# Token halves at the turn from one residual stage to the next stage's first products, in a two-layer decoder trunk on one Trainium2 core

## The chip, the cores and the metric

The kernel runs on one core of a Trainium2 chip. Its time is the device time of that core, in microseconds (us). Five engines take part, each with its own instruction order and joined by semaphores: PE (TensorE, the matmuls), ACT (ScalarE), VectorE (DVE), POOL (GpSimd) and SP (SyncE, which issues the DMAs).

## What is computed

512 tokens of 1024 features pass through two layers. Each layer has a token mixer (an HGRN2 gated recurrence, then FoX, attention with a forget gate) and an MLP with squared ReLU, each between a conditioned norm and a gated residual update:

```python
def rmsnorm(x, w):
    return x * lax.rsqrt(jnp.mean(x * x, axis=-1, keepdims=True) + EPS) * w
def modulate(x, w, shift, scale):
    return rmsnorm(x, w) * (1 + scale) + shift
# layer i
h = modulate(x, norm1_w[i], sh1, sc1)
y = hgrn2_mixer(h, ...) if i % 2 == 0 else fox_mixer(h, ...)      # ends in "@ w_out"
x = x + g1 * y
h = modulate(x, norm2_w[i], sh2, sc2)
a = relu(h @ w1[i]); x = x + g2 * ((a * a) @ w2[i])               # 4096 wide inside
# at the end
rmsnorm(x, final_w)
```

## The kernel before

**Layout.** Everything between stages is feature-major: x holds 8 tiles (k = 0 to 7) of 128 features by 512 tokens. Each product is made in three matmuls of fp32r, from an upper and a lower part of either side (upper by upper, upper by lower, lower by upper; `product`, L620, the matmuls at L624 to L626).

**Weights.** All large weights lie in one stream of 208 blocks of 128 x 1024 values, four blocks to a quad. A quad's block j has slot j of three buffers: `raw` (filled by SP, L233), `whi` (the upper part, made by ACT in `hi_ahead`, L283 to L287) and `wlo` (raw less whi, made by POOL in `lo`, L544 to L547). `hi_ahead(quad, j)` waits until PE is through with block j of that quad (`pe_blk`) and until raw holds block j of the next one; `lo` waits for it, SP reloads raw behind `lo`, and PE's `split` (L617) waits for both parts. Layer 0 has quads 0 to 25 and layer 1 quads 26 to 51: 8 for the mixer's input, 2 for w_out, 16 for the MLP. The MLP goes in two halves of four quads w1 and four quads w2, so that in the second half the last four quads (12 to 15 of the MLP) are w2. A w_out tile takes one block, a w2 tile takes two.

**Residual stage.** With each tile that PE finishes, VectorE updates x from the PSUM bank (L1178), ACT squares the tile into `sqb` (L380) and VectorE adds it to `acc` (L1188); PE's next use of the bank waits for the update (`x_upd`). ACT's `residual` (L370) does, for each quad:

```python
for j in range(4):
    if not last and j < 3:
        hi_ahead(q0 + q, j)
    if j % per == per - 1:      # per: blocks a tile, 1 at w_out, 2 in the MLP
        ...                     # square of the tile
    if not last and j == 3:
        hi_ahead(q0 + q, j)
```

**Norm.** After the last tile `norm` of PE (L636) sums acc and the last square over the features with a column of 1/1024 (L641, L646). VectorE adds epsilon (L997), POOL takes the power -1/2 (L551), PE spreads it over the partitions (L651). Then, tile by tile, VectorE scales x into one of two buffers (L1008), ACT adds the shift and rounds to the upper part (L293) and VectorE makes the lower part (L1013). PE's next products start with each k as it lands: `together` (L704) takes two blocks at once, FoX alternates the forget gate's product (L936 to L938) with token blocks of 256 columns (L679 to L681). There are five norms; norm 0 is at the start, 1 and 3 follow w_out, 2 and 4 the MLPs. Norm 4 is the last: VectorE scales x in place (L1339) and SP stores each tile (L277).

**Behind norm 2.** The forget gate's product is followed by ACT's absolute value, exponential and logarithm (L414 to L418), VectorE's scan (L1236), and the trip of the result through DRAM. In ACT's order the weights' upper parts for FoX's next blocks stand behind this. q and k are squared, summed over a head (L1242), rooted on POOL (L551) and scaled (L1253) before PE turns them (L879) and begins the scores (L894).

## Time and profile before

| | us |
|---|---|
| median of 3 runs | 1496.41 |
| lowest and highest | 1494.38, 1497.65 |
| span of the profiled execution | 1490.3 |
| PE busy in it | 1416.5 (95%) |
| VectorE busy | 753.5 (51%) |
| POOL busy | 687.3 (46%) |
| ACT busy | 506.8 (34%) |

The profile gives the span from the first to the last instruction of one execution; that execution's own time is not listed beside it, so the median is read as 6.1 us above the span. Busy PE is not PE at its peak, since matmuls overlap: what counts is the distance from one start to the next. A matmul row shows its start, its duration with the drain, the line, and the tiles it writes and reads; "x8" merges eight alike. The bracket at a row's end is how long the engine had been idle and what released it.

### The profile page before, as it was taken

What the parts mean: (1) busy time and instruction counts of PE and PEld (TensorE: products, weight loads), DVE (VectorE), ACT (ScalarE), POOL (GpSimd) and SP (SyncE); (2) the same over time, 40 slices, a digit from 0 to 9 for tenths busy, and PEclk for the clock granted to TensorE, in tenths of its full rate; (3) what the DMA queues carried; (4) which work ended last, traced back from release to release, by engine and by line L of the source; (5) the groups of instructions that cost most, each with busy time, mean ns of one, the idle gap of its engine ahead of it and who ended that gap; (6) DMA issues with size and microseconds to landing.
All of it is one profiled execution on the core that took longest, in us unless ns stands there. A gap on an engine that the chain in (4) does not pass through costs nothing.

```text
span 1490.3 us, 20799 instructions
## 1 busy us (share of the span) xinstructions
PE 1416.5 (95%) x7488; PEld 1186.5 (80%) x7488; DVE 753.5 (51%) x1087; ACT 506.8 (34%) x750; POOL 687.3 (46%) x399
## 2 busy tenths in 40 slices
PE   2789999999899999999998999999989999999997
PEld 2678988988788888888787888888778888888885
DVE  7764656464698457871253333333356541255312
ACT  3513232313343223332245353534234332233220
POOL 8456758474355455554434333333053444444440
PEclk9889999999899999999999999999999999999998
DMA  9233433322265456542323121211032223222221
GB/s 380 101 141 114 141 114 118 137 72 70 87 225 197 169 181 214 197 165 89 99 68 103 57 86 57 86 58 57 15 104 80 89 95 99 85 99 99 85 70 57
DMA packets 46192, 169.83 MB, mean 114 GB/s; under 512 B 5024, under 2 KB 5152, under 8 KB 45360
## 3 DMA queue, kind: packets, MB, share of 16 engines
q1 hardware_dynamic: 45520, 164.73, 32.0%
q10 hardware_dynamic: 608, 4.23, 0.8%
q8 instruction: 43, 0.70, 0.2%
q14 instruction: 21, 0.17, 0.0%
HBM read 166.81 MB, written 2.13 MB: 113 GB/s over the span
## 4 chain that ended last, share of the span: by engine, by line
PE 66%; issue 19%; POOL 8%; DVE 5%; ACT 1%; DMA 1%; POOLq 0%; DVEq 0%; ACTq 0%; SPq 0%
PE bank L624 13%; PE bank L625 13%; PE bank L626 13%; POOL wlo L547 8%; PE bank L679 4%; PE bank L681 4%; PE bank L680 4%; PE bank L752 3%; PE bank L894 3%; PE bank L918 2%; PE bank L771 1%; PE bank L905 1%; DVE modf L1073 1%; PE bank L896 1%; DVE mring L1033 1%
## 5 line engine op out<-in xcount | busy, mean ns | idle before, releaser
L547 POOL TENSOR_TENSOR wlo<-raw,whi 128x1024 fp32r<-128x1024 f32 x208 | 539.2, 2596 | 661.5 <-ACT whi L287 661.5
L287 ACT ACTIVATE whi<-raw 128x1024 fp32r<-128x1024 f32 x204 | 215.1, 1055 | 211.3 <-PE bank L626 187.5
L1178 DVE SCALAR_TENSOR_TENSOR x<-bank,mod,x 128x512 f32<-128x512 f32 (+1 forms) x48 | 35.9, 749 | 234.6 <-PE bank L626 234.6
L1033 DVE CUSTOM_DVE_ANT_0 mring<-mring,cb 128x1024 f32<-128x1024 f32 x80 | 124.9, 1570 | 4.0 <-DMA mring<-mod_rows 4.0
L679 PE MATMUL bank<-whi,h2hi 128*128 128x256 f32 x384 | 111.3, 290 | 0.0
L1266 DVE CUSTOM_DVE_ANT_0 scr<-bank,fb 128x128 f32<-128x128 f32 (+1 forms) x64 | 31.1, 486 | 153.7 <-issue 153.7
L681 PE MATMUL bank<-wlo,h2hi 128*128 128x256 f32 x384 | 108.5, 283 | 0.0
L680 PE MATMUL bank<-whi,h2lo 128*128 128x256 f32 x384 | 108.4, 282 | 0.0
L398 ACT ACTIVATE scr<-bank 128x512 f32<-128x512 f32 x64 | 38.2, 597 | 196.4 <-PE bank L626 196.4
L624 PE MATMUL bank<-h3hi,whi 128*128 128x512 f32 x256 | 102.1, 399 | 2.4 <-issue 2.4
L624 PE MATMUL bank<-h1hi,whi 128*128 128x512 f32 x256 | 100.9, 394 | 2.4 <-DVE h1lo L1013 2.4
L625 PE MATMUL bank<-h3lo,whi 128*128 128x512 f32 x256 | 101.7, 397 | 0.0
L626 PE MATMUL bank<-h3hi,wlo 128*128 128x512 f32 x256 | 101.7, 397 | 0.0
L625 PE MATMUL bank<-h1lo,whi 128*128 128x512 f32 x256 | 101.3, 396 | 0.0
L625 PE MATMUL bank<-a1lo,whi 128*128 128x512 f32 x256 | 101.0, 395 | 0.0
L624 PE MATMUL bank<-a1hi,whi 128*128 128x512 f32 x256 | 101.0, 395 | 0.0
L626 PE MATMUL bank<-a1hi,wlo 128*128 128x512 f32 x256 | 101.0, 395 | 0.0
L624 PE MATMUL bank<-a0hi,whi 128*128 128x512 f32 x256 | 100.7, 393 | 0.3
L626 PE MATMUL bank<-h1hi,wlo 128*128 128x512 f32 x256 | 100.8, 394 | 0.0
L625 PE MATMUL bank<-a0lo,whi 128*128 128x512 f32 x256 | 100.1, 391 | 0.0
L626 PE MATMUL bank<-a0hi,wlo 128*128 128x512 f32 x256 | 99.9, 390 | 0.0
L624 PE MATMUL bank<-h0hi,whi 128*128 128x512 f32 x192 | 81.7, 426 | 15.6 <-DVE h0lo L1013 15.3
(231 smaller groups left out, 3158.3 us busy)
## 6 DMA issues: line engine op xcount, KB each, us to landing
raw<-stream SPq DMA_DIRECT2D x208, 512.0 KB, 3.5
mring<-mod_rows SPq DMA_DIRECT2D x80, 512.0 KB, 3.5
modf<-mod_rows SPq DMA_DIRECT2D x8, 1024.0 KB, 18.1
fb<-negf ACTq DMA_DIRECT2D x4, 1024.0 KB, 5.5
x<-x_t SPq DMA_DIRECT2D x2, 1024.0 KB, 7.0
out_t<-x SPq DMA_DIRECT2D x8, 256.0 KB, 2.1
cb<-c_row SPq DMA_DIRECT2D x1, 512.0 KB, 4.1
wf<-w_forget SPq DMA_DIRECT2D x1, 512.0 KB, 4.3
```

Of the source, the lines that this page charges most:

```text
L287: S.activation(whi[:, j, :], raw[:, j, :], ACT.Copy).then_inc(w_hi, 1)
L398: S.activation(scr[j % 2][:, :], ps[j][:, :], ACT.Relu).then_inc(ff_r, 1)
L547: G.tensor_tensor(wlo[:, j, :], raw[:, j, :], whi[:, j, :].bitcast(F32), ALU.subtract).then_inc(w_lo, 1)
L624: PE.matmul(out, wh, hh[0], start=first, stop=False)
L625: PE.matmul(out, wh, hh[1], start=False, stop=False)
L626: return PE.matmul(out, wl, hh[0], start=False, stop=last)
L679: PE.matmul(o, hh, whi[:, j, w0], start=k == 0 and t % 2 == 0, stop=False, skip_group_check=True)
L680: PE.matmul(o, hl, whi[:, j, w0], start=False, stop=False, skip_group_check=True)
L681: mm = PE.matmul(o, hh, wlo[:, j, w0], start=False, stop=k == KT - 1, skip_group_check=True)
L752: mm = PE.matmul(second_halves(cols(ps[j], t), m), cols(kk, t), second_halves(cols(qq, t), m), start=True, stop=True)
L894: PE.matmul(o[:, 0:n], qkT[0][r:r + DH, f, P * i:P * i + P], qkT[1][r:r + DH, f, 0:n], start=True, stop=False, skip_group_check=True)
L1033: V.tensor_tensor_reduce(out=mring[:, s, :], in0=mring[:, s, :], in1=cb[:, :], scale=1.0, scalar=0.0, op0=ALU.mult, op1=ALU.add, accum_out ...
```

## The change

In each of the four turns (n = 1 to 4, after w_out and MLP of each layer) the last quad of the residual stage runs twice over its four blocks, first for tokens 0 to 255, then for tokens 256 to 511. Norm n is done by such halves (`sums`, `spread`, `variance`, `half_root`, `normed_tokens`); the sums and the spread of half 0 stand inside the last quad's second round, those of half 1 inside the first quad of the next stage, which also goes by token halves. Scaled tiles have four buffers of 256 tokens. The last norm's output is stored in pairs of half tiles. The squares of the MLPs' first halves, which were summed and never used, are gone, and so are the memsets of `acc`: the first square of a stage is written into it. ACT's and VectorE's `residual` and `norm` become a `turnover` each, written out, where ACT's order of weight conversions and squares is new. In SBUF h1 now lies ahead of a0, and h2 ahead of FoX's other tiles.

```diff
+        h1 = [sb(n, [P, KT, T], F32R, mlp0) for n in ("h1hi", "h1lo")]
         a0 = [sb(n, [P, HALF, T], F32R, mlp0) for n in ("a0hi", "a0lo")]
-        h1 = [sb(n, [P, KT, T], F32R, mlp0) for n in ("h1hi", "h1lo")]
         wf = sb("wf", [P, D], F32, mlp0)
...
         fox = ExitStack()
+        h2 = [sb(n, [P, KT, T], F32R, fox) for n in ("h2hi", "h2lo")]
...
+        OUT_UPD, MLP_UPD, LAST_UPD = 12, 8, 10
+        UPD_AT = [0, 12, 20, 30, 42, 50]
...
-                sp.wait_ge(out_t_ready, k + 1)
-                sp.dma_start(out_t[:, k, :], x[:, k, :]).then_inc(out_done, 16)
+            for th in range(2):
+                for k in range(0, KT, 2):
+                    sp.wait_ge(out_t_ready, KT * th + k + 2)
+                    sp.dma_start(out_t[:, k:k + 2, part(th)], x[:, k:k + 2, part(th)]).then_inc(out_done, 16)
             sp.wait_ge(out_done, 16 * KT)
 
...
+            def upper(n, th, first, end, h, shift):
+
+                for k in range(first, end):
+                    act.wait_ge(h_t, h_at(n, th, k))
+                    S.activation(h[0][:, k, part(th)], t_buf(th, k), ACT.Identity,
                                  bias=mod[:, shift + k:shift + k + 1]).then_inc(h_hi, 1)
...
+            def square(n, upd, i, add, t, cols_, dst):
+
+                act.wait_ge(x_upd, upd)
+                act.wait_ge(x_acc, add)
+                S.activation(dst[:, cols_], x[:, t, cols_], ACT.Square).then_inc(x_sq, 1)
+
+            def square_half(n, th, t):
+
+                r, full_ = (0, 4) if from_w_out(n) else (2, 6)
+                upd = UPD_AT[r + 3 * (n > 2)] + full_ + (KT - full_) * th + t - full_ + 1
+                add = ADD_AT[n] + full_ - 1 + (KT - full_ - 1) * th + t - full_
+                square(n, upd, 0, add, t, part(th), sqb)
 
             act.wait_ge(c_in, 16)
...
+            def turnover(n, q0, h, shift):
+
+                all_ = slice(0, T)
+                if from_w_out(n):
                     for j in range(4):
...
+                        hi_ahead(q0, j)
+                        square(n, UPD_AT[3 * (n > 2)] + j + 1, 0, ADD_AT[n] + max(j - 1, 0), j, all_, sqb if j else acc)
+                    q0 += 1
+                else:
+                    for t in range(6):
+                        square(n, UPD_AT[2 + 3 * (n > 2)] + t + 1, 0, ADD_AT[n] + max(t - 1, 0), t, all_, sqb if t else acc)
+                        if t % 2:
+                            for j in ((0, 1, 2, 3)):
+                                hi_ahead(q0 + t // 2, j)
+                    q0 += 3
+                last_ = range(4, KT) if from_w_out(n) else range(6, KT)
+                for t in last_:
+                    square_half(n, 0, t)
+                if from_w_out(n):
+                    for j in range(2):
+                        square_half(n, 1, 4 + j)
+                        hi_ahead(q0, j)
+                    upper(n, 0, 0, 3, h, shift)
+                    square_half(n, 1, 6)
+                    hi_ahead(q0, 2)
+                    upper(n, 0, 3, 6, h, shift)
+                    square_half(n, 1, 7)
+                    hi_ahead(q0, 3)
+                else:
+                    if n == 4:
+                        square_half(n, 1, 6)
+                        square_half(n, 1, 7)
+                        return
+                    hi_ahead(q0, 0)
+                    square_half(n, 1, 6)
+                    hi_ahead(q0, 1)
+                    upper(n, 0, 0, 3, h, shift)
+                    hi_ahead(q0, 2)
+                    upper(n, 0, 3, 6, h, shift)
+                    square_half(n, 1, 7)
+                    hi_ahead(q0, 3)
+                upper(n, 0, 6, KT, h, shift)
+                upper(n, 1, 0, KT, h, shift)
...
+                    if half == 0:
+                        with act.Fori(0, 4) as q:
+                            for j in range(4):
+                                hi_ahead(q + base + 4, j)
+                turnover(2 * layer + 2, base + 12, h, shift)
+
...
+            def half_root(n, th):
+
+                root(n_var, norm_at(n, th), 2, n_rst, 2 * th)
+
             def lo_quads(first, end, n):
 
                 with pool.Fori(first, end - 1) as q:
                     for j in range(4):
                         lo(q, j)
+                half_root(n, 0)
                 for j in range(4):
-                    if j == 3:
-                        root(n_var, n, TT, n_rst)
                     lo(end - 1, j)
-
-            lo_quads(Q_OUT + 1, Q_OUT + 3, 2)
-            lo_quads(Q_MLP + 1, LAYER_QUADS + 1, 3)
+                half_root(n, 1)
...
+            def half_block(quad, j, out, h, th, k0=0, first=True, last=True, between=None):
+
+                if th == 0:
+                    split(quad, j)
+                for k in range(KT):
+                    mm = product(out[:, part(th)], j, k, [h[0][:, k0 + k, part(th)], h[1][:, k0 + k, part(th)]],
+                                 first and k == 0, last and k == KT - 1)
+                    if between is not None and k in between:
+                        between[k]()
+                return mm
+
...
+            def sums(n, th):
+
+                bank = ps[SUMS_BANK[n][th]]
+                pe.wait_ge(x_acc, adds_at(n, th))
+                pe.wait_ge(x_sq, squares_at(n, th))
+                for i in range(2):
+                    PE.matmul(bank[:, i:i + 1], cols(acc, 2 * th + i), meand[:, 0:1], start=i == 0, stop=False,
+                              skip_group_check=True)
+                for i in range(2):
+                    mm = PE.matmul(bank[:, i:i + 1], cols(sqb, 2 * th + i), meand[:, 0:1], start=False, stop=True,
+                                   skip_group_check=True)
+                mm.then_inc(n_sum, 1)
+
+            def spread(n, th):
+
+                bank = ps[SPREAD_BANK[n][th]]
+                pe.wait_ge(n_rst, norm_at(n, th))
+                for i in range(2):
+                    mm = PE.matmul(cols(bank, i), rst[:, 2 * th + i:2 * th + i + 1].broadcast_to([P, P]), ident[:, :],
+                                   start=True, stop=True)
...
+            def w_out(quad, y, y_done, upd0, n):
                 pe.wait_ge(*y_done)
                 for j in range(4):
                     for k in range(EARLY, KT):
                         mm = product(ps[4 + j][:, :], j, k, [y[0][:, k, :], y[1][:, k, :]], False, k == KT - 1)
                     mm.then_inc(pe_blk, 1)
                 for j in range(4):
+                    half_block(quad + 1, j, ps[j], y, 0).then_inc(pe_half, 1)
+                for j in range(4):
                     pe.wait_ge(x_upd, upd0 + j + 1)
-                    feature_block(quad + 1, j, 4 + j, y)
+                    between = {5: lambda: sums(n, 0)} if j == 0 else None
+                    half_block(quad + 1, j, ps[4 + j], y, 1, between=between).then_inc(pe_blk, 1)
+                    if j == 1:
+                        pe.wait_ge(x_upd, upd0 + 9)
+                        spread(n, 0)
 
...
+                            for pair in range(2):
+                                for k in range(KT):
+                                    if pair == 0:
+                                        pe.wait_ge(h_lo, h_at(n, th, k))
+                                    for j in (2 * pair, 2 * pair + 1):
+                                        if th == 0 and k == 0:
+                                            split(base, j)
+                                        mm = product(ps[j][:, part(th)], j, k, [h[0][:, k, part(th)], h[1][:, k, part(th)]],
+                                                     k == 0, k == KT - 1)
+                                        if th == 1 and k == KT - 1:
+                                            mm.then_inc(pe_blk, 1)
+                                    if th == 0 and k == 3:
+                                        (sums, spread)[pair](n, 1)
                         first = 1
                     with pe.Fori(first, 4) as q:
...
-            w_out(Q_OUT, y0, (y_lo, KT), 0)
-            norm(1)
+                quad, n = base + 15, 2 * layer + 2
+                for th in range(2):
+                    for j in range(4):
+                        out = ps[(0, 6)[th] + j // 2]
+                        between = {5: lambda: sums(n, 0)} if th and j == 0 else None
+                        mm = half_block(quad, j, out, a, th, k0=KT * (j % 2), first=j % 2 == 0, last=j % 2 == 1,
+                                        between=between)
+                        if th:
+                            mm.then_inc(pe_blk, 1)
+                        elif j % 2:
+                            mm.then_inc(pe_half, 1)
+                        if th and j == 1:
+                            spread(n, 0)
...
+            def token_half(n, bank, th, k):
+
+                j = (n + k // 4) % 4
+                if th == 0 and k % 4 == 0:
+                    split((n + k // 4) // 4, j)
+                w0 = slice(GW * (k % 4), GW * (k % 4) + GW)
+                for t in (2 * th, 2 * th + 1):
+                    o = ps[bank + th][:, GW * (t % 2):GW * (t % 2) + GW]
+                    hh, hl = cols(h2[0][:, k, :], t), cols(h2[1][:, k, :], t)
+                    PE.matmul(o, hh, whi[:, j, w0], start=k == 0 and t % 2 == 0, stop=False, skip_group_check=True)
+                    PE.matmul(o, hl, whi[:, j, w0], start=False, stop=False, skip_group_check=True)
+                    mm = PE.matmul(o, hh, wlo[:, j, w0], start=False, stop=k == KT - 1, skip_group_check=True)
+                if th and k % 4 == 3:
+                    mm.then_inc(pe_blk, 1)
...
-                for k in (2 * kk, 2 * kk + 1):
-                    pe.wait_ge(h_lo, 2 * KT + k + 1)
+            for th in range(2):
+                for k in range(KT):
+                    pe.wait_ge(h_lo, h_at(2, th, k))
+                    token_half(4 * L, 4, th, k)
                     wh, wl = cols(wfs[0], k), cols(wfs[1], k)
-                    PE.matmul(ps[0][:, :], wh, h2[0][:, k, :], start=k == 0, stop=False)
-                    PE.matmul(ps[0][:, :], wh, h2[1][:, k, :], start=False, stop=False)
-                    mm = PE.matmul(ps[0][:, :], wl, h2[0][:, k, :], start=False, stop=k == KT - 1)
-                if kk == KT // 2 - 1:
+                    PE.matmul(ps[0][:, part(th)], wh, h2[0][:, k, part(th)], start=k == 0, stop=False)
+                    PE.matmul(ps[0][:, part(th)], wh, h2[1][:, k, part(th)], start=False, stop=False)
+                    mm = PE.matmul(ps[0][:, part(th)], wl, h2[0][:, k, part(th)], start=False, stop=k == KT - 1)
+                    if th == 0 and k == 3:
+                        sums(2, 1)
+                if th:
                     mm.then_inc(f_pe, 1)
-                fox_half(-1, 4 + kk)
-            for i in range(8, 16):
+                for k in range(KT):
+                    token_half(4 * L + 2, 6, th, k)
+                    if th == 0 and k == 1:
+                        spread(2, 1)
+            for i in range(12, 16):
...
+            def variance(n, th):
+
+                dve.wait_ge(n_sum, norm_at(n, th))
+                eps_var(ps[SUMS_BANK[n][th]][:, 0:2], 2, 2 * th).then_inc(n_var, 1)
+
+            def normed_tokens(n, th, first, end, h, shift):
+
+                if first == 0:
+                    dve.wait_ge(n_bc, norm_at(n, th))
+                for k in range(first, end):
+                    if KT * th + k >= 4:
+                        dve.wait_ge(h_lo, h_at(n, th, k) - 4)
+                    V.scalar_tensor_tensor(out=t_buf(th, k), in0=x[:, k, part(th)],
+                                           scalar=gain[:, KT * n + k:KT * n + k + 1],
+                                           in1=ps[SPREAD_BANK[n][th]][:, 0:TH], op0=ALU.mult, op1=ALU.mult).then_inc(h_t, 1)
+                for k in range(first, end):
+                    dve.wait_ge(h_hi, h_at(n, th, k))
+                    V.scalar_tensor_tensor(out=h[1][:, k, part(th)], in0=t_buf(th, k),
+                                           scalar=mod[:, shift + k:shift + k + 1],
+                                           in1=h[0][:, k, part(th)].bitcast(F32), op0=ALU.add,
+                                           op1=ALU.subtract).then_inc(h_lo, 1)
...
+            def update(t, bank, cols_, gate):
+
+                V.scalar_tensor_tensor(out=x[:, t, cols_], in0=ps[bank][:, cols_], scalar=mod[:, gate + t:gate + t + 1],
+                                       in1=x[:, t, cols_], op0=ALU.mult, op1=ALU.add).then_inc(x_upd, 1)
+
+            def added(square_at, cols_):
+
+                dve.wait_ge(x_sq, square_at)
+                V.tensor_tensor(acc[:, cols_], acc[:, cols_], sqb[:, cols_], ALU.add).then_inc(x_acc, 1)
+
+            def turnover(n, q0, gate, half0, h, shift):
+
+                all_ = slice(0, T)
+                full_ = 4 if from_w_out(n) else 6
+                per = 1 if from_w_out(n) else 2
+                for t in range(full_):
+                    dve.wait_ge(pe_blk, 4 * q0 + per * (t + 1))
+                    update(t, 4 + t % (4 // per), all_, gate)
+                    if t:
+                        added(SQ_AT[n] + t + 1, all_)
+                for t in range(full_, KT):
+                    dve.wait_ge(pe_half, half0 + t - full_ + 1)
+                    update(t, t - full_, part(0), gate)
+                    if t < KT - 1:
+                        added(SQ_AT[n] + t + 1, part(0))
+
+                def second(t):
+                    dve.wait_ge(pe_blk, 4 * q0 + per * (t + 1))
+                    update(t, (4 if from_w_out(n) else 6) + t - full_, part(1), gate)
+                    if t < KT - 1:
+                        added(SQ_AT[n] + KT + t - full_ + 1, part(1))
+
+                variance(n, 0)
+                if n == 4:
+                    second(6)
+                    finished(0)
+                    second(7)
+                    variance(n, 1)
+                    finished(1)
+                    return
+                if from_w_out(n):
+                    second(4)
+                    second(5)
+                else:
+                    second(6)
+                normed_tokens(n, 0, 0, 3, h, shift)
+                if from_w_out(n):
+                    second(6)
+                normed_tokens(n, 0, 3, 6, h, shift)
+                second(7)
+                normed_tokens(n, 0, 6, KT, h, shift)
+                variance(n, 1)
+                for k in range(0, KT, 2):
+                    normed_tokens(n, 1, k, k + 2, h, shift)
```

## Rows read from the trace of the kernel before

**Rows 1.** Windows of layer 1's MLP; busy us and instructions of each engine, then clock, DMA
```profile
1140.00:1450.00 310.00, 310.00 (x1336) 251.34 (x1335) 119.49 (x87) 97.11 (x128) 134.52 (x57) 1.00 0.28 92
```

**Rows 2.** PE's timeline after w_out of layer 0: start us, us, line, operands
```profile
378.07 0.95 PE L641 MATMUL bank<-meand,acc 128*128 128x1 f32 x8
...
382.29 2.07 PE L651 MATMUL bank<-ident,rst 128*128 128x128 f32 x8 [1.34 <-POOL rst L551]
386.75 0.80 PE L624 MATMUL bank<-h1hi,whi 128*128 128x512 f32 x1 [2.38 <-DVE h1lo L1013]
...
391.13 0.39 PE L625 MATMUL bank<-h1lo,whi 128*128 128x512 f32 x1
...
399.84 0.39 PE L624 MATMUL bank<-h1hi,whi 128*128 128x512 f32 x1
```

**Rows 3.** PE's timeline after w_out of layer 1
```profile
1109.24 0.94 PE L641 MATMUL bank<-meand,acc 128*128 128x1 f32 x8
...
1113.47 1.16 PE L651 MATMUL bank<-ident,rst 128*128 128x128 f32 x8 [1.34 <-POOL rst L551]
1117.06 0.76 PE L624 MATMUL bank<-h3hi,whi 128*128 128x512 f32 x1 [2.43 <-issue]
```

**Rows 4.** Timeline at the end of layer 0's MLP
```profile
741.21 0.95 PE L641 MATMUL bank<-meand,acc 128*128 128x1 f32 x8
741.41 0.75 DVE L1178 SCALAR_TENSOR_TENSOR x<-bank,mod,x 128x512 f32<-128x512 f32 x1 [6.90 <-PE bank L626]
```

**Rows 5.** PE's timeline from there to FoX's first scores
```profile
749.49 0.77 PE L936 MATMUL bank<-h2hi,wfhi 128*128 128x512 f32 x1 [2.47 <-DVE h2lo L1013]
...
768.18 0.28 PE L679 MATMUL bank<-whi,h2hi 128*128 128x256 f32 x1
...
774.06 0.28 PE L680 MATMUL bank<-whi,h2lo 128*128 128x256 f32 x1
...
796.05 0.46 PE L894 MATMUL bank<-kT,qT 64*128 64x128 f32 x2 [0.87 <-ACT kT L455]
```

**Rows 6.** Timeline at the span's end, PE and VectorE
```profile
1476.11 0.95 PE L641 MATMUL bank<-meand,acc 128*128 128x1 f32 x8
...
1480.17 2.08 PE L651 MATMUL bank<-ident,rst 128*128 128x128 f32 x8 [1.34 <-POOL rst L551]
...
1482.29 5.36 DVE L1339 SCALAR_TENSOR_TENSOR x<-x,par,bank 128x512 f32<-128x512 f32 x8 [2.71 <-PE bank L651]
```

**Rows 7.** Timeline between two quads of layer 0's second w2 half
```profile
719.23 0.39 PE L624 MATMUL bank<-a0hi,whi 128*128 128x512 f32 x1
...
719.65 0.75 DVE L1178 SCALAR_TENSOR_TENSOR x<-bank,mod,x 128x512 f32 x1 [7.11 <-PE bank L626]
...
720.61 0.63 ACT L380 ACTIVATE sqb<-x 128x512 f32 x1 [5.61 <-DVE x L1178]
...
721.15 1.04 ACT L287 ACTIVATE whi<-raw 128x1024 fp32r<-128x1024 f32 x1
...
722.27 2.42 POOL L547 TENSOR_TENSOR wlo<-raw,whi 128x1024 fp32r<-128x1024 f32 x1 [4.80 <-ACT whi L287]
```

**Rows 8.** VectorE's groups by form: xcount, busy us, mean ns, idle before
```profile
L1188 DVE TENSOR_TENSOR acc<-acc,sqb 128x512 f32<-128x512 f32 x44 | 59.3, 1349 | 32.6 <-ACT sqb L380 32.6
...
L1178 DVE SCALAR_TENSOR_TENSOR x<-bank,mod,x 128x512 f32<-128x512 f32 x24 | 17.9, 747 | 69.1 <-PE bank L626 69.1
...
L1275 DVE COPY pT<-bank 128x512 f32<-128x512 f32 x16 | 11.1, 692 | 4.9 <-PE bank L905 3.2
...
L1275 DVE COPY pT<-bank 128x256 f32<-128x256 f32 x16 | 6.7, 420 | 0.0
```

**Rows 9.** VectorE's timeline, FoX's first quads, then the kernel's start
```profile
777.39 5.69 DVE L1253 TENSOR_TENSOR qt<-qt,rst 128x512 f32<-128x512 f32 x2 [3.02 <-POOL rst L551]
...
40.60 2.14 DVE L1013 SCALAR_TENSOR_TENSOR h0lo<-scr,mod,h0hi 128x512 fp32r<-128x512 f32 x1
```

**Rows 10.** POOL's timeline behind the forget gate
```profile
771.11 3.23 POOL L547 TENSOR_TENSOR wlo<-raw,whi 128x1024 fp32r<-128x1024 f32 x1 [23.41 <-ACT whi L287]
```

197 lines of the change are left out of this document (82 added, 115 removed).

## Prediction

> **What bounds the kernel now.** The page and the windows by stage come first: in a long stretch of the MLPs PE is busy in all 310 us of 310, so there only PE's own work counts. [rows 1] PE stands still elsewhere: at the four places where a residual stage ends and a norm stands between it and the next product, so I read PE's timeline around each. After w_out of layer 0 the last long matmul gives way to the sums at 378.07, the spread runs at 382.29, the first product of the norm's output starts at 386.75, and the first two blocks end at 399.84. [rows 2] Two blocks of 24 matmuls at 0.229 us are 11.0 us, so 21.8 - 11.0 = 10.8 us are lost: 8.7 us of gap, and about 2 us since ten matmuls from 386.75 on take 4.4 us for 2.3 (a granted clock of 1.2 instead of 2.4 GHz). After w_out of layer 1 the gap is 7.8 us and the loss, with the same slow restart, about 10.0. [rows 3] After the MLP of layer 0 the gap is 8.3 us. [rows 4, 5] The last norm has nothing behind it: from 1476.11 to the span's end are 14.2 us. [rows 6] These four losses are all that the split of the last quad can win.
>
> **What the change does to PE's work.** A block of 24 matmuls of 512 columns becomes 48 of 256: 8 blocks at each w_out turn, 5 at the first MLP's (the forget gate's product counts as one), 4 at the end, 25 in all, 600 pairs. Matmuls of 256 columns (FoX's token blocks) start every (774.06 - 768.18) / 49 = 0.120 us [rows 5], so a pair costs 0.240 for 0.229: 600 x 0.011 = 6.6 us more. The Trainium skill (TensorE: Matmul & The Clock Gate, section Back-to-back issue gap) gives columns / 2.4 GHz plus 2.5 ns between matmuls; by that the split would cost 600 x 2.5 ns = 1.5 us, and I go by the rows. Sums (8 short matmuls) and spread (4) now stand in PE's stream, 0.84 + 0.49 us a half by their pitch of 0.105 and 0.12; they are in the schedules below. That a0 and h1 trade places, and h2 moves, I cost at nothing: they keep the token half that is being written off tiles still read, and the pitch is 0.229 whichever tile streams.
>
> **The step that decides: weights behind the odd squares.** ScalarE rounds each raw block into its upper part (hi_ahead), POOL then makes the lower one, and a slot can be refilled once PE has read it. Before, hi_ahead of slots 0 to 2 runs right after each block, with three blocks of cover. In the new ACT turnover of the MLPs, the loop over t = 0 to 5 takes the square of t first and converts all four slots only if t is odd, (0, 1, 2, 3). Square 1 waits for update 1, which waits for the fourth block of the quad. So no slot of the next quad is started before this quad is wholly done, and its block 0 has no cover. The trace has this very chain, for the slot that came last: PE goes on to the next quad at 719.23, update 719.65, square 720.61, upper part 721.15, lower part 722.27 to 724.69: 5.5 us. [rows 7] There it delayed nothing, since slot 3 is needed 16 us later; now slot 0 is behind it and PE waits. In code without the loop's register work the update starts 0.20 us after PE, not 0.42 [rows 4], so I take 5.3. The other slots follow every 2.4 us and PE needs one every 5.5, or 2.9 in halves, so it is one wait a quad: before quads 13, 14 and 15 of each MLP, 6 x 5.3 = **31.8 us**. The bounds are 5.0 and 5.6 (30 and 34 in all): no row lets the chain be shorter. The clock: at two of three turns it was down 4.1 to 4.2 us after the last long matmul (8 spreads took 2.07 and 2.08 us, at the third 1.16) [rows 2, 3, 6], and a restart then cost 2.1 us; while here PE has not even the short matmuls in between. I take 1.5 us a wait, nearer to that row than to nothing, **9.0** in all, between 0 and 13.
>
> **The four turns, worked as a schedule.** Halved durations are the 512-wide ones less 0.27 on VectorE, as its copies of 512 and 256 columns show (0.692 and 0.420 us) [rows 8]: update, scaling and lower part 0.48 us, addition 0.43. Square 0.42 is an estimate, a third off the 0.63 of rows 7, less than VectorE's copies lose; upper part 0.51 and root 0.69 likewise, and an error of 0.1 in each moves a turn by 0.3. Added to it is a collision. VectorE instructions that read two SBUF tensors wait while POOL makes a lower part: additions mean 1.35 us for 0.69 alone, two adjacent multiplies took 5.69 together for 1.4, room for two lower parts by POOL of 2.4 each ahead of them, and a lower part of h0 took 2.14 for 0.75. Updates, which read PSUM and SBUF, never do (mean 0.75). [rows 8, 9] The new order puts POOL's four lower weights (2.4 us each) among VectorE's lower halves of h. With T the start of the second halves of a w_out turn: sums of half 0 at T + 2.2, root 3.4, spread after block 1 at 6.6. The lower part of k = 0 waits behind POOL until 11.4, just in time for PE at 12.9. Then k = 3 is behind POOL's third block (14.9 to 17.3) and lands at 17.7, when PE has been idle since 15.0; the sums of half 1 wait for the last square until 19.8; k = 6 is behind POOL's fourth (to 23.1) and lands at 23.6. The second token half is in time. In all 6.4 us idle and 48.7 of work, 55.1 us from the start of the last quad to the end of the next stage's first quad. Before: 22.0 + 10.8 + 22.0 = 54.8. So **+0.3** at the first turn, and against 54.0 **+1.1** at layer 1's: the norm's gap is given back.
>
> After layer 0's MLP the products end at 57.1 after the quad's start, for 60.5 before. But the forget gate's product now ends with the second token half, at 51.4 instead of 46.1. Behind it are ScalarE's two table loads, the upper part for the next block, VectorE's scan and POOL's lower part, which ended at 774.34, 55.1 after the quad's start. [rows 10] Shifted by 5.3 it is ready at 60.4: PE waits from 57.1. The normalised q, ready at 783.1 (63.8) [rows 9], comes at 69 and PE wants it at 66; k's follows. The first scores, at 796.05 or 76.8 before [rows 5], start at 81.5: **+4.7**.
>
> At the end, half 0's scaling is hidden, half 1 goes through update, square, sums, root, spread and eight scalings of 0.40: the last ends 31.7 after the quad's start. Before it was 22.0 + 11.5; from there to the span's end 2.65 us stay (the stores' bytes are the same). [rows 6] 34.4 for 36.2: **-1.8**.
>
> **Edits costed at nothing.** The MLPs' first halves lose eight squares and additions a layer, and the memsets of acc go: work of ACT and VectorE beside a PE that doesn't wait there [rows 1], so no gain either. SP issues as many stores as before, eight of two tiles' halves in place of eight whole tiles, and its raw loads keep their place behind the lower parts; a raw slot has the rest of a quad, over 16 us, to fill, and if that were gone PE would wait for the load as well. POOL runs each root ahead of the lower weights that follow it; the roots are short, and VectorE's variance ahead of them doesn't wait for those weights.
>
> **Sum.** 31.8 + 9.0 + 0.3 + 1.1 + 4.7 - 1.8 = 45.1 us. The profiled execution's span of 1490.3 becomes 1535.4; the median of the three runs, 6.1 above that span, becomes 1541.5.
>
> **Rivals.**
> 1. The clock does not fall in the six waits: 1541.5 - 9.0 = 1532.5. For it: after layer 1's w_out the spread, 4.2 us in, still ran at the full clock (8 matmuls in 1.16 us) [rows 3]. Against: 2.07 and 2.08 us for the same 8 at two other turns. [rows 2, 6] Chance 0.22.
> 2. The collision with POOL does not bite (it finds gaps between VectorE's shorter instructions). The same schedules without it give 48.9 for the w_out turns, 73.0 for the scores: -5.9 - 5.1 - 3.8 - 1.8 = -16.6 instead of +4.3, so 1520.6. Against it are rows that show the very pair of operations. [rows 8, 9] Chance 0.14.
> 3. Not slower: the conversion before each quad is hidden after all. With rival 2's turns at -16.6, it decides from the point where the six waits and their clock cost under 2.8 us each; at nothing the time is 1479.8. That needs ACT to convert slot 0 before square 1, which the order of its instructions forbids. Chance 0.04.
> 4. The clock stays down through the halved blocks too, a fall costing 3 us instead of 1.5 and one more of 2 at each of three turns: +9 and +6, 1556.5. Chance 0.08.
>
> **Numbers.** Forecast 0.52, the rivals as above. The range takes in rivals 1 and 2 and the forecast's own bounds (the waits at 5.6, the clock at 13): 1520 to 1553. About 0.2% is what a measurement of this kernel can tell from no change: faster 0.03, same 0.01, slower 0.96.
>
> **What would show it.** Right: six gaps of PE of 5.0 to 5.6 us in the second halves of the MLPs, ended by POOL's wlo, each some 22 us after the last, and a granted clock below 1 in the slices around; at the w_out turns gaps of 1 to 3 us ended by the lower parts of h while POOL is busy; the first block after the forget gate held by wlo. Wrong: no wait of PE for wlo at those quads, or a norm turn shorter than before by 5 us.

## The result, and the profile after

The median of four runs after is 1536.20 us (1534.91 to 1538.62), of four runs before 1497.02: ratio 1.0264, 95% interval 1.0245 to 1.0284, so 39 us slower. The forecast was 1541.5 in a range of 1520 to 1553. The profiled execution took 1534.91 us, its span 1532.9: 42.6 us more than the span before. The span is what is split up here; that it grew by 3 us more than the median comes from the trace before, as e8_places will show.

Windows of the changed kernel over its two second w2 halves, from the first quad to the end of the halved quad's first round. Columns as in [rows 1].

```profile
653.00:753.00 100.00, 84.94 (x397) 71.08 (x396) 15.01 (x23) 17.79 (x23) 31.21 (x13) 0.91 0.23 72
1410.00:1511.00 101.00, 86.08 (x399) 71.65 (x398) 12.38 (x16) 17.47 (x22) 30.49 (x13) 0.92 0.16 51
```

Where PE was busy all the time at a clock of 1.00 [rows 1], it now stands still for 15 us in each stretch, at a mean granted clock of 0.91 and 0.92. The page's groups of instructions name what ended that idle time, the same for both layers:

```profile
L704 PE MATMUL bank<-a0hi,whi 128*128 128x512 f32 (+1 forms) x288 | 109.4, 380 | 15.2 <-POOL wlo L622 14.9
L704 PE MATMUL bank<-a1hi,whi 128*128 128x512 f32 (+1 forms) x288 | 109.5, 380 | 14.9 <-POOL wlo L622 14.9
```

The timeline at the first of the six places, quad 12 to quad 13 of layer 0:

```profile
673.71 0.39 PE L706 MATMUL bank<-a0hi,wlo 128*128 128x512 f32 x1
674.14 0.75 DVE L1335 SCALAR_TENSOR_TENSOR x<-bank,mod,x 128x512 f32<-128x512 f32 x1 [10.23 <-PE bank L706]
674.92 0.63 ACT L336 ACTIVATE sqb<-x 128x512 f32<-128x512 f32 x1 [10.35 <-DVE x L1335]
675.46 3.88 ACT L323 ACTIVATE whi<-raw 128x1024 fp32r<-128x1024 f32 x4
...
676.58 7.00 POOL L622 TENSOR_TENSOR wlo<-raw,whi 128x1024 fp32r<-128x1024 f32 x3 [20.07 <-ACT whi L323]
679.07 0.76 PE L704 MATMUL bank<-a0hi,whi 128*128 128x512 f32 x1 [4.97 <-POOL wlo L622]
...
679.63 0.63 PE L705 MATMUL bank<-a0lo,whi 128*128 128x512 f32 x1
...
683.90 0.62 PE L706 MATMUL bank<-a0hi,wlo 128*128 128x512 f32 x1
684.33 0.43 PE L704 MATMUL bank<-a0hi,whi 128*128 128x512 f32 x1
684.59 0.39 PE L705 MATMUL bank<-a0lo,whi 128*128 128x512 f32 x1
```

It is the chain of [rows 7], now for all four slots: the quad's last matmul, update, square, then four upper parts in a row, and PE goes on once the first lower part is made. From start to start 5.36 us lie between the two matmuls, 0.23 of it the matmul itself: 5.13 us lost. Behind the wait eleven matmuls start 0.43 us apart instead of 0.23, the lower of the clock's two levels, and cost 2.5 us more. The six waits are 5.13 or 5.14 us each; their slow matmuls cost 2.5, 1.4 and 2.3 us in layer 0, 2.6, 1.4 and 2.1 in layer 1, 12.4 us in all. After the middle wait of each layer some 5 matmuls were slow, after the others 10 or more.

PE's timeline can be cut into stretches, each around one turn; their lengths in us:

| stretch | before | after | difference |
|---|---|---|---|
| n=1: w_out of layer 0 to the first product over a | 129.0 | 127.4 | -1.6 |
| n=2: layer 0's second w2 half to the first scores | 143.1 | 166.9 | +23.8: waits 15.4, their clock 6.3, the turn +2.1 |
| FoX: first scores to w_out | 282.4 | 283.3 | +0.8 |
| n=3: w_out of layer 1 to the first product over a | 129.9 | 129.0 | -0.9 |
| n=4: layer 1's second w2 half to the span's end | 103.4 | 123.7 | +20.3: waits 15.4, their clock 6.1, the turn -1.3 |

With 0.3 us ahead of the first of them, that makes the 42.6. The rest of the MLPs is unchanged.

VectorE, POOL and PE after w_out of layer 0. The kernel before has no counterpart, since its norm stood alone there:

```profile
376.23 2.41 POOL L622 TENSOR_TENSOR wlo<-raw,whi 128x1024 fp32r<-128x1024 f32 x1 [0.43 <-ACT whi L323]
377.18 2.54 DVE L1188 SCALAR_TENSOR_TENSOR h1lo<-scr,mod,h1hi 128x256 fp32r<-128x256 f32 x3
...
381.59 2.36 POOL L622 TENSOR_TENSOR wlo<-raw,whi 128x1024 fp32r<-128x1024 f32 x1 [2.95 <-ACT whi L323]
382.11 2.91 DVE L1188 SCALAR_TENSOR_TENSOR h1lo<-scr,mod,h1hi 128x256 fp32r<-128x256 f32 x3
384.28 0.38 PE L704 MATMUL bank<-h1hi,whi 128*128 128x256 f32 x1 [1.83 <-DVE h1lo L1188]
```

Each time VectorE's group of three ends 1.1 us after POOL's block (378.64 to 379.72, 383.95 to 385.02), two lower parts' time or a little more: so the first one ends about when the block does, and PE waits for it. PE's line at the turn after layer 0's MLP:

```profile
798.31 0.55 PE L791 MATMUL bank<-whi,h2hi 128*128 128x256 f32 x1 [3.27 <-POOL wlo L622]
...
816.96 0.66 PE L1017 MATMUL bank<-ident,kt 128*128 128x128 f32 x4 [3.24 <-DVE kt L1467]
818.48 0.76 PE L1032 MATMUL bank<-kT,qT 64*128 64x128 f32 x2 [0.87 <-ACT kT L531]
```

### The profile page after: what moved, and what is told of

Its sections match the earlier page's. It is cut to its first block, busy times and chain, and to the rows that moved or that the text cites. A ratio compares the mean times of both kernels' runs of the same rounds, so it can differ in the third digit from the quotient of the medians.

```text
span 1532.9 us, 21793 instructions
## 1 busy us (share of the span) xinstructions
PE 1432.9 (93%) x8088; PEld 1224.4 (80%) x8088; DVE 739.6 (48%) x1136; ACT 501.5 (33%) x770; POOL 690.6 (45%) x403
## 4 chain that ended last, share of the span: by engine, by line
PE 41%; issue 33%; POOL 16%; DVE 7%; ACT 2%; DMA 1%; POOLq 0%; DVEq 0%; SPq 0%; ACTq 0%
POOL wlo L622 15%; PE bank L704 6%; PE bank L706 6%; PE bank L705 6%; PE bank L791 3%; PE bank L793 3%; PE bank L792 3%; PE bank L864 3%; PE bank L1032 3%; PE bank L1056 2%; PE bank L883 1%; PE bank L1043 1%; DVE modf L1239 1%; PE bank L1034 1%; DVE h2lo L1188 1%
## 5 line engine op out<-in xcount | busy, mean ns | idle before, releaser
L704 PE MATMUL bank<-a0hi,whi 128*128 128x512 f32 (+1 forms) x288 | 109.4, 380 | 15.2 <-POOL wlo L622 14.9
L704 PE MATMUL bank<-a1hi,whi 128*128 128x512 f32 (+1 forms) x288 | 109.5, 380 | 14.9 <-POOL wlo L622 14.9
L704 PE MATMUL bank<-h3hi,whi 128*128 128x512 f32 (+1 forms) x288 | 107.5, 373 | 2.2 <-DVE h3lo L1188 2.1
L704 PE MATMUL bank<-h1hi,whi 128*128 128x512 f32 (+1 forms) x288 | 107.1, 372 | 2.2 <-DVE h1lo L1188 2.1
L705 PE MATMUL bank<-a1lo,whi 128*128 128x512 f32 (+1 forms) x288 | 108.7, 377 | 0.0
L706 PE MATMUL bank<-a1hi,wlo 128*128 128x512 f32 (+1 forms) x288 | 108.7, 377 | 0.0
L706 PE MATMUL bank<-a0hi,wlo 128*128 128x512 f32 (+1 forms) x288 | 107.9, 375 | 0.0
L705 PE MATMUL bank<-a0lo,whi 128*128 128x512 f32 (+1 forms) x288 | 107.7, 374 | 0.0
L706 PE MATMUL bank<-h3hi,wlo 128*128 128x512 f32 (+1 forms) x288 | 107.0, 371 | 0.0
L705 PE MATMUL bank<-h3lo,whi 128*128 128x512 f32 (+1 forms) x288 | 106.9, 371 | 0.0
```

Source lines behind the costliest of these rows:

```text
L704: PE.matmul(out, wh, hh[0], start=first, stop=False)
L705: PE.matmul(out, wh, hh[1], start=False, stop=False)
L706: return PE.matmul(out, wl, hh[0], start=False, stop=last)
```

## Experiments on the six waits

**e1_order.** Only the order of ScalarE in the MLPs' turnover is put back:

```diff
 for t in range(6):
+    for j in ((0, 1), (2,))[t % 2]:
+        hi_ahead(q0 + t // 2, j)
     square(...)
-    if t % 2:
-        for j in ((0, 1, 2, 3)):
-            hi_ahead(q0 + t // 2, j)
+    for j in ((), (3,))[t % 2]:
+        hi_ahead(q0 + t // 2, j)
```

> The changed kernel with one thing put back: in the six early squares of each MLP's turnover, ScalarE makes the upper parts of slots 0 and 1 ahead of the even square, that of slot 2 ahead of the odd one and that of slot 3 behind it. Theory A (this order alone makes the six waits of PE, and the clock's fall behind them is part of their price): the trace of the changed kernel has 6 x 5.13 = 30.8 us of gap before quads 13, 14 and 15 of each MLP and 12.5 us of slow matmuls behind them, so 1536.2 - 43.3 = 1493, that is 3 to 4 us under the kernel before; no gap of PE for wlo there. Theory B (the raw blocks or POOL's queue are late as well, and the order only showed it first): waits of 1 us or more stay at these quads, and the time is over 1500.

Measured: 1494.15 us, ratio to before 0.9985 (0.9972 to 0.9998): 42 of the 43 us are back, and the kernel is 1.7 us under the one before that ran beside it, where 3 to 4 were expected. The windows of the same two stretches:

```profile
653.00:731.00 78.00, 77.86 (x393) 65.86 (x392) 19.03 (x23) 18.92 (x23) 32.38 (x13) 1.00 0.30 93
1390.00:1469.00 79.00, 79.00 (x396) 66.51 (x395) 15.73 (x16) 17.92 (x22) 31.20 (x13) 1.00 0.20 63
```

PE is busy throughout at a clock of 1.00. All the rest of the change (halves, norms within products, places) is worth 0.15%, with an interval from 0.02 to 0.28.

**e2_slot0.** As above, but with `((0,), ())` ahead of the square and `((), (1, 2, 3))` behind it.

> The changed kernel with only slot 0's upper part made early (ahead of the even square); slots 1 to 3 are still made behind the odd square, when the quad is done. Theory A (one wait a quad, slot 0's; the later slots have blocks of PE's in front of them): slot 1's lower part lands 5.1 us after the quad, as slot 0's did; PE wants it after 5.5 us in whole blocks (no wait) and after 2.8 us in the halved last quad (a wait of 2.3 us, twice), so some 5 us more than with the whole order put back, plus a clock fall of up to 2 us each: 1493 + 5 to 9 = 1498 to 1502. Theory B (the wait moves to slot 1 in every quad, since POOL and the clock are as late as before): three quarters or more of the loss stays, 1525 or more.

Measured: 1498.11 us, 1.0014 (1.0004 to 1.0024), 4.0 us over e1_order. PE's timeline has no wait before quads 13 and 14, and in the halved quad one at slot 1:

```profile
725.20 0.36 PE L705 MATMUL bank<-a0hi,whi 128*128 128x256 f32 x1 [2.26 <-POOL wlo L623]
```

By the starts that is 2.41 us, and 2.29 at the same place of layer 1, against 2.3 expected: a wait is 5.1 us less the cover that the slot has, 0 for slot 0, 2.8 or 5.5 us for slot 1.

**e3_old_late.** The kernel before, with both squares of the three inner quads ahead of all four `hi_ahead`.

> The kernel before, with whole quads and whole norms, in which the three inner quads of each MLP's second w2 half make the upper parts of all four slots behind both squares. Theory A (the order alone, whatever the halves do): six waits of 5.1 to 5.3 us, 31 us, and the slow matmuls behind them, 12 us: 1497 + 43 = 1540, slower than the changed kernel itself by the 3 to 4 us that the halves win. Theory B (the halved last quads or the moved tiles have a part in the waits or in the clock's fall): 1497 + 20 to 30, under 1530.

Measured: 1542.26 us, 1.0296 (1.0273 to 1.0319). One of its six waits:

```profile
681.74 0.77 PE L637 MATMUL bank<-a0hi,whi 128*128 128x512 f32 x1 [5.38 <-POOL wlo L560]
```

With the loop's register work ahead of the update each wait is 5.5 us, as [rows 7] had it; the slow matmuls cost 1.8, 2.5 and 2.8 us in layer 0, 1.4, 2.1 and 2.5 in layer 1. The kernel is 46 us over the one before that ran beside it, where 43 were expected. The loss needs nothing of the halves.

**e4_filled.** The changed kernel; at the end of each quad of the second w2 half:

```diff
+if half:
+    pe.wait_ge(x_upd, q * 2 + (UPD_AT[3 * layer + 2] + 1))
+    for _ in range(20):
+        PE.matmul(ps[4][:, :], a[0][:, 0, 0:P], a[0][:, 0, :], start=True, stop=True)
```

> The changed kernel, in which PE runs 20 matmuls of 512 columns that nobody reads (a tile of a as both operands, into a bank that is free) in each of the six waits: 20 x 0.229 = 4.6 us, inside the 5.13 us. Theory A (the slow matmuls behind the waits are the clock, which falls because PE stands still): the gap shrinks to some 0.5 us, the next quad comes at the same time, and the slow matmuls go: 1536.2 - 12.5 = 1524, the granted clock over the kernel from 0.973 up to 0.98. Theory B (the matmuls behind the wait are slow because their weights or data have just been written, not for the clock): no change, 1536.

Measured: 1526.30 us, 1.0196 (1.0178 to 1.0215), 9.9 us under the changed kernel. PE around the first place, and the two windows:

```profile
675.27 4.71 PE L978 MATMUL bank<-a0hi 128*128 128x512 f32 x20
680.46 0.47 PE L704 MATMUL bank<-a0hi,whi 128*128 128x512 f32 x1 [0.48 <-POOL wlo L622]
680.78 0.39 PE L705 MATMUL bank<-a0lo,whi 128*128 128x512 f32 x1
...
653.00:748.00 95.00, 93.42 (x459) 77.91 (x458) 15.60 (x23) 19.04 (x24) 31.54 (x13) 1.00 0.25 78
1408.00:1503.00 95.00, 93.58 (x458) 77.78 (x457) 12.01 (x16) 17.10 (x22) 30.75 (x13) 1.00 0.17 52
```

The wait is as long (5.19 from the first added matmul to the next useful one), but the matmuls behind it start 0.23 us apart and the clock is 1.00. So the slow matmuls come from PE's pause, not from fresh weights, and waits of 5.1 us do bring the clock down here each time. The traces have nearly all of it in these stretches (from the first w2 matmul to the end of the halved quad's first round 101.5 to 95.6 us in layer 0, 102.0 to 96.3 in layer 1: 11.6 in all); in the medians 2.5 of the 12.4 us are missing, and no run says where.

**e8_places.** The kernel before, with h1 allotted ahead of a0 and h2 first in its stage.

> The kernel before with nothing but the SBUF places of the change (h1 ahead of a0, h2 at the front of its stage). Theory A (a place costs nothing): 1496 within 3 us, the matmuls over a0, h1 and h2 start every 0.229 us in layer 0 as before. Theory B (the pitch hangs on the tile's place, or a transfer or a copy now meets another): over 0.2% in either direction, and the pitch of one of the tiles another by more than 0.001 us.

Measured: 1495.55 us, ratio 1.0000 (0.9986 to 1.0014); the matmuls over h1 and a0 start every 0.2289 us. Places cost nothing.

This run also says how much a single trace can carry. Its instructions stand in the order of the kernel before, and yet its span is 1493.3 us for 1490.3 and its stretches are 129.0, 144.4, 283.5, 130.7 and 103.4 us for 129.0, 143.1, 282.4, 129.9 and 103.4. Against it the changed kernel's span is 39.6 us longer, as the medians have it (39.2); the turn at n=2 is then +0.8 us and not +2.1, FoX -0.2, n=3 -1.7. A difference of 1 or 2 us between two single traces is not the change's for certain.

## Experiments on the turns

All of these stand on e1_order.

**e7_no_collision.** In the last quad of `lo_quads`, POOL subtracts only the first 8 of a slot's 1024 columns; at three turns, that leaves nearly all of 12 blocks of lower weights out of the computation.

> On the kernel with the order put back (1494.2 us), with part of the work left out: of the last quad of POOL's lower parts at the three turns (after both w_out and after layer 0's MLP, 12 blocks) only 8 of 1024 columns are made, so that POOL is hardly busy while VectorE makes the lower halves of h. Theory A (at the turns VectorE's instructions with two SBUF tensors stand still while POOL makes a block, and PE's gaps there are this): the groups of three lower halves of 2.5 to 5.1 us fall to 1.3 us, PE's gaps of 1.9, 0.9 and 0.5 us at each w_out turn go, with them 1.1 us of slow matmuls, and about 1 us after the MLP: 1494.2 - 4.4 - 4.4 - 1 = 1484 to 1486. Theory B (the gaps come from the order of VectorE's and ScalarE's queues): under 2 us are won in all, and the groups stay over 2 us.

Measured: 1482.51 us, 0.9907 (0.9883 to 0.9931). VectorE after w_out of layer 0, the same groups:

```profile
377.37 1.27 DVE L1190 SCALAR_TENSOR_TENSOR h1lo<-scr,mod,h1hi 128x256 fp32r<-128x256 f32 x3
...
381.03 1.27 DVE L1190 SCALAR_TENSOR_TENSOR h1lo<-scr,mod,h1hi 128x256 fp32r<-128x256 f32 x3
```

By stretches, against e1_order, n=1 wins 5.1, n=3 5.5 and n=2 1.0 us, and no gap of PE is left at the w_out turns. The collision is the whole of them.

**e10_hold_h.** The same collision avoided with nothing left out:

```diff
 for j in range(4):
+    if j:
+        pool.wait_ge(h_lo, h_at(n, 0, (2, 5, 7)[j - 1]))
     lo(end - 1, j)
```

> On the kernel with the order put back (1494.2 us): at the three turns with a stage behind them POOL makes slot 1's lower part only when the lower halves of h up to k = 2 are made, slot 2's after k = 5, slot 3's after k = 7. Theory A (the collision is what PE's gaps at the turns are, as leaving the blocks out showed with 4.9 us at the first w_out turn, 5.5 at the second and 1.0 after the MLP): the groups of three lower halves take 1.3 us, the gaps of 1.9, 0.9 and 0.5 us go, slot 3 is late by at most 0.7 us in their place: 3.5 to 4.5 us less at each w_out turn and 0 to 1 after the MLP, 1485 to 1487. Theory B (POOL's four blocks, held back, come too late for the second pair of blocks and PE waits as long for wlo): within 2 us of 1494.

Measured: 1485.69 us, 0.9925 (0.9909 to 0.9941), and by stretches -2.9 (n=1), -3.5 (n=3) and -1.0 us (n=2). POOL starts a block when VectorE's group of lower parts is through, and both run at full pace:

```profile
377.30 1.27 DVE L1191 SCALAR_TENSOR_TENSOR h1lo<-scr,mod,h1hi 128x256 fp32r<-128x256 f32 x3
...
378.64 2.41 POOL L623 TENSOR_TENSOR wlo<-raw,whi 128x1024 fp32r<-128x1024 f32 x1 [2.73 <-DVE h1lo L1191]
```

**e5_slot0_ahead.** `hi_ahead(LAYER_QUADS, 0)` stands ahead of the forget gate's Abs, Exp and Ln.

> On the kernel with the order put back (1494.2 us): ScalarE makes the upper part of slot 0 behind FoX's first block ahead of the forget gate's Abs, Exp and Ln instead of behind them. Theory A (two things wait on the forget gate's chain, and the later one sets the first scores: k's normalisation, for which PE stood 3.24 us): the 3.3 us wait of PE for slot 0's lower part goes, slot 1's takes its place with about 3 us, and the first scores stay at 797.1 within 0.5 us: 1494 within 1. Theory B (PE's wait for the lower part is worth its length, as the prediction's step had it): 3.3 us and the slow matmuls behind it, 1.3 us, go: 1489.5.

Measured: 1491.22 us, 0.9972 (0.9959 to 0.9986). In PE's timeline the wait of 3.3 us for the first lower part is down to 0.9 us, for another cause, and the next one, for q's turn, has grown from 1.17 to 4.15 us:

```profile
774.52 0.38 PE L792 MATMUL bank<-whi,h2hi 128*128 128x256 f32 x1 [0.92 <-ACT qt L520]
784.62 1.11 PE L1018 MATMUL bank<-ident,qt 128*128 128x128 f32 x4 [4.15 <-DVE qt L1468]
...
796.60 0.46 PE L1033 MATMUL bank<-kT,qT 64*128 64x128 f32 x2 [0.87 <-ACT kT L533]
```

From the second w2 half to the scores it is 144.7 us for 145.1. So theory A holds where the edit acts, though the wait that took over was q's and not slot 1's. The median fell by 2.9 us all the same; in the trace that is 1.2 us in FoX and 0.9 in layer 1's turn, which the edit doesn't touch, at a granted clock of 0.985 over the kernel against 0.983. The intervals of the two ratios overlap, and I don't count it. The medians of e6_q_ahead and e9_hold_qk lie as near (1491.35 and 1491.25), and their intervals touch e1_order's too, so for these three runs the stretch to the scores decides.

**e6_q_ahead.** FoX's first two blocks on ScalarE, and `sums(0, 0)` on VectorE, stand ahead of the forget gate's chain.

> On the kernel with the order put back (1494.2 us): the slots' upper parts behind FoX's first two blocks and q's squares and copies on ScalarE, and q's sums on VectorE, stand ahead of the forget gate's chain, which takes 4.6 us of ScalarE and has time until the first softmax. Theory A (that chain ahead of q is what holds both the weights and q and k): q's and k's normalisations come some 5.5 us earlier, PE's own work ends at 787.5 and k's turn is the last to be waited for, first scores at 791 for 797.1, 6 us less and up to 1 more for the clock: 1487.5 to 1488.5. Theory B (the two multiplies of 5.6 us beside POOL's lower parts set the pace whenever they start, or the forget gate's output now comes late for the softmax): under 2 us are won, 1492.5 or more.

Measured: 1491.35 us, 0.9960 (0.9945 to 0.9974), between the two theories; the stretch to the scores takes 142.0 us for 145.1. ScalarE's timeline shows what neither had:

```profile
776.92 0.64 ACT L540 ACTIVATE gs<-gs 128x512 f32<-128x512 f32 x1
780.25 0.35 ACTq L542 DMA_DIRECT2D negf<-gs  x1
780.74 1.06 ACT L323 ACTIVATE whi<-raw 128x1024 fp32r<-128x1024 f32 x1 [3.18 <-DVE gs L1513]
...
782.77 0.60 ACT L512 ACTIVATE sqb<-bank 128x512 f32<-128x512 f32 x1 [0.97 <-DMA negf<-gs]
```

k's squares stand behind the wait for the forget gate's output and for a transfer, and PE then waits 6.0 us for k's turn. q's two multiplies, which POOL left alone this time, took 1.27 us; k's took 5.57:

```profile
780.14 1.27 DVE L1460 TENSOR_TENSOR qt<-qt,rst 128x512 f32<-128x512 f32 x2
...
788.78 5.57 DVE L1460 TENSOR_TENSOR kt<-kt,rst 128x512 f32<-128x512 f32 x2 [3.02 <-POOL rst L627]
...
794.41 1.12 PE L1018 MATMUL bank<-ident,kt 128*128 128x128 f32 x4 [6.04 <-DVE kt L1460]
```

**e9_hold_qk.** POOL waits until `f_nrm`, which counts VectorE's multiplies of q and k, is 2 before slot 2's lower part and 4 before slot 3's: first q's two, then k's two.

> On the kernel with the order put back (1494.2 us): POOL waits for q's two multiplies before it makes slot 2's lower part, and for k's two before slot 3's, in FoX's first quad; nothing else. Theory A (k's normalisation sets the first scores, and its multiplies take 5.6 us for 1.3 only because POOL makes lower parts beside them): k's group falls to 1.3 us, the first scores come at 792.6 to 793.5 for 797.1, since PE's own work ends at 791 then: 4 us less, 1490. Theory B (the multiplies are slow by themselves, or slots 2 and 3 now come late): k's group stays above 3 us or PE waits for wlo behind the first scores, and the time is 1494 within 1.5.

Measured: 1491.25 us, 0.9959 (0.9943 to 0.9975). VectorE's k group, PE's turn of k and the first scores:

```profile
789.44 1.29 DVE L1470 TENSOR_TENSOR kt<-kt,rst 128x512 f32<-128x512 f32 x2 [3.01 <-POOL rst L627]
...
793.93 0.63 PE L1020 MATMUL bank<-ident,kt 128*128 128x128 f32 x4 [2.35 <-ACT qT L532]
...
795.43 0.47 PE L1035 MATMUL bank<-kT,qT 64*128 64x128 f32 x2 [0.87 <-ACT kT L532]
```

k's multiplies fell from 5.6 to 1.3 us, and the stretch to the scores from 145.1 to 142.3. That is 1 us less of a gain than expected: PE then waits 2.35 us for ScalarE's copy of q's turn out of the one bank.

**e11_all.** e1, e6, e9 and e10 together, and k's block ahead of `act.wait_ge(f_out, 1)`.

> Everything together: the order put back, POOL's waits at q, k and at the turns, q's squares and sums ahead of the forget gate's chain, and k's squares on ScalarE ahead of its wait for that chain's output (with q ahead alone, ScalarE stood at that wait from 777.6 to 780.7 and on to 782.8 for a transfer before it took k's squares). Theory A: k's multiplies end near 788, as PE ends its own work, first scores 7 us before those of the kernel with the order put back; the turns 7 to 9 us less: 1494.2 - 7 - 8 = 1479, at most 1481. Theory B (the gains share one limit, or the clock takes them back): 1485 or more.

Measured: 1477.18 us, 0.9867 (0.9848 to 0.9885), faster than the kernel before that ran beside it by 20 us and than the changed one by 59, and 2 us under what was expected. The stretch to the scores is 135.8 us for 143.1 before, the w_out stretches are 4.5 and 3.7 us shorter than before.

## Why the prediction was right

The kernel is slower for the reason that was given, the six waits of PE behind the odd squares and the clock's fall after them: these make 43.2 us, where the span grew by 42.6 in all. The smaller terms were further off, and partly cancel each other.

**The six waits** (31.8 us): 30.8, each 5.13 for 5.3. The update followed PE by 0.20 us as taken, and the square came 0.78 us behind it for 0.96 in [rows 7]. e1, e2 and e3 show that the order alone is the cause, and slot 0 nearly the whole of it. Rival 3, the hidden conversion, is out with that.

**The clock** (9.0, between 0 and 13): 12.4, near the upper bound. That it falls was right; the size "1.5 us a wait" was too small: 2.1 to 2.6 at four of the six, 1.4 at the middle ones. Rival 1 (no fall) is out by the trace and by e4; rival 4 (3 us a fall) is out too, since none cost over 2.6.

**The split** (6.6 by rows, 1.5 by the Trainium skill, TensorE: Matmul & The Clock Gate, section Back-to-back issue gap): in between. The section gives its formula for the isolated matmul; it makes 0.216 us of 512 columns and 0.109 of 256, and the traces don't agree, with 0.2289 and 0.1178 in layer 0. Halved matmuls of the changed kernel, 49 rows and then 53:

```profile
356.36 0.28 PE L704 MATMUL bank<-y0hi,whi 128*128 128x256 f32 x1
...
361.80 0.35 PE L704 MATMUL bank<-y0hi,whi 128*128 128x256 f32 x1
...
363.40 0.28 PE L705 MATMUL bank<-y0lo,whi 128*128 128x256 f32 x1
...
369.52 0.28 PE L706 MATMUL bank<-y0hi,wlo 128*128 128x256 f32 x1
```

In the later rows 6.12 us for 52 starts are 0.1177 us, in layer 1 it is 0.119; a pair is then 0.006 over the whole matmul in either layer, 600 x 0.006 = 3.6 us. In the earlier rows 5.44 us for 48 starts are 0.1133 us, and a pair costs no more than the whole matmul. So 3.6 is an upper estimate, and the 0.120 of FoX's token blocks was too high a row: the same blocks start every 0.119 us from 786.02 on in the trace before. No run tells what sets the pitch.

**The w_out turns** (+0.3, +1.1): -1.6 and -0.9, so the sign was wrong at both, and a small part of the norm's gap is won after all. The mechanism was right, block for block; 6.4 us of idle were too many (the waits written out in the schedule add up to 5.6 only). POOL's third block began 14.1 us into the second halves for 14.9 and its fourth 19.4 for 20.7. Every matmul was a little quicker and the last square earlier, so PE waited 1.8, 0.8 and 0.2 us behind k = 3, the sums and k = 6, where 2.7, 1.3 and 1.6 were forecast. Against that stands a term that the schedule left out: the clock falls here too. Most halved matmuls of this window start 0.213 us apart, which costs about 1.1 us at each of the two turns:

```profile
386.00:390.90 4.90, 4.66 (x26) 4.38 (x27) 2.97 (x4) 1.61 (x3) 3.08 (x2) 0.65 0.19 77
```

Rival 2 (no collision) is out: without the collision these turns are 5.1 and 5.5 us shorter, as e7 measured.

**The turn after layer 0's MLP** (+4.7): +2.1 against the trace before, +0.8 against e8_places. Two waits stand there as forecast in length, 3.3 us for the lower part and 3.2 at a turn; but the second is k's and not q's, for which PE waits 0.2 us. e5 shows that the first of them costs nothing by itself. The kernel before already waited 2.35 us there, which the schedule didn't name:

```profile
794.55 0.63 PE L879 MATMUL bank<-ident,kt 128*128 128x128 f32 x4 [2.35 <-ACT qT L455]
```

The size that was off is the shift of the forget gate's chain, 5.3 us in the schedule. Counted from the halved quad's start, and less the 2.3 us of slow matmuls behind the wait, its lower part lands at 58.6 us for 55.1 before: 3.5 us. **The end** (-1.8): -1.3.

**The sum** came to 45.1 for 42.6 by the two spans: waits -1.0, clock +3.4, w_out turns -3.9, the third turn with FoX -1.8, the end +0.5, the start +0.3. Against e8_places it is 45.1 for 39.6, with -4.7 for the w_out turns and -4.1 for the third turn with FoX, and this is the better base. The 52 executions of the kernel before that ran beside the experiments are all 1.7 or 1.8 us longer than their spans; so the one traced before, with its span of 1490.3, took some 1492 us and was 5 us shorter than the median, and what the prediction read as 6.1 us between span and median is mostly this. By the medians the forecast was 5.3 us high because its sum was 5.9 too large (45.1 for 39.2) and its base 0.6 too low. That it came so near is partly luck: the clock was put 3.4 us too low and the three norm turns between 5.7 and 8.8 us too high.

## What to carry to other kernels

When a loop is rewritten so that an engine does its work for the next stage behind its work for this one, look for the instruction of the next stage that has no cover: here one of four slots, six times, took 43 us with the clock, where the same delay of the other three slots alone costs 4. Price a wait of TensorE with its restart: 5.1 us of pause cost another 1.4 to 2.6. Where two engines slow each other down, a wait that puts one behind the other can be a gain (8.5 us in e10_hold_h; 2.8 us of the stretch to the scores in e9_hold_qk). And where terms of 1 or 2 us are to be told apart, one trace of each kernel is too few.

## What the runs showed of the hardware that was not expected

The same pause of 5.13 us cost 1.4 us of slow matmuls at the middle quad of each layer and 2.1 to 2.6 at the others, in both layers alike. It isn't the quad's place: in e3_old_late, with pauses of 5.5 us, the first of each layer was the cheapest (1.8 and 1.4 us). What sets it no run tells. Filling the pause with matmuls that nobody reads kept the clock at 1.00 and won 10 of the 12 us, for 120 added matmuls.

The lower parts of h, VectorE's instructions with two SBUF operands, don't slow down evenly beside POOL's subtraction, they stand nearly still until it ends: three of them took 2.54 and 2.91 us with a block beside them, 1.27 without, while POOL's block took 2.4 us either way. It can also go the other way round. Here a block of POOL begins 0.2 us behind VectorE's scan; the scan takes its usual 1.2 us and the block 3.18:

```profile
794.79 1.23 DVE L1450 TENSOR_TENSOR_SCAN gs<-prob,scr 128x512 f32<-128x512 f32 x1
794.99 3.18 POOL L622 TENSOR_TENSOR wlo<-raw,whi 128x1024 fp32r<-128x1024 f32 x1 [21.52 <-ACT whi L323]
```

So the later one waits, in these rows.
